# mLSTM layer on one core: the order of the opening, where two weight products stand, and the gate arithmetic in ten pieces

## The chip, the cores and the metric

The kernel runs on one core of a Trainium2 chip. The metric is device time in microseconds (us) of one execution, median over the runs shown. Engines are named as in the profile: PE (matrix products and transposes), PEld (its weight loads), DVE (vector), ACT (activation), POOL (GpSimd), SP (issues most loads).

## The reference, cut to what matters

One layer (DEPTH 1, so only the mLSTM mixer and the SwiGLU run), 2048 tokens, width 1024, 8 heads:

```
u = rmsnorm(x, mix_norm_g)
q, k, v, o_pre, if_pre = split(u @ w_in)          # 3072 columns, and 16 gate columns
gates = if_pre + b_if;  log_i = gates[:8];  log_f = log_sigmoid(gates[8:])
# per chunk: cumulated log_f, running maximum m, decay matrix, scores, state (C, n)
h = x + (rmsnorm_heads(h_mlstm) * norm_g * sigmoid(o_pre)) @ w_out
out = h + (silu(rms(h) @ w_gate) * (rms(h) @ w_up)) @ w_down
```

## The kernel before

**Arithmetic.** Every float32 matrix is kept as a high and a low part (both of a reduced float32 format): a product is three passes on PE, high x low, high x high, low x high. ACT makes the high part by a copy, DVE the low part by a subtraction. Over that lies Strassen's scheme in Winograd's form: a 2 x 2 block product takes 7 products (P1 to P7) of sums of blocks. On the side of the tokens these sums are T1 to T4 of early token tiles (0 to 3 of a half) and late ones (4 to 7).

**Halves and stages.** The tokens are done in two halves (h = 0, 1) of 8 tiles of 128. Each half: opening (norm, transposes, split), input projection (84 units, 12 groups of 7 products), the recurrence over 8 chunks, the SwiGLU's up phase, and its down phase (77 units, e = 0 to 76). The opening of half 1 follows on the down phase of half 0: rows of half 1 are normed beside units 36 to 71 (ROWS_AT), one pair is summed at unit 52 (SUMS_AT) and tiles 0 to 3 are transposed beside units 69 to 72 (TURN_AT). Half 0 has no such phase ahead of it.

**The opening.** A half has 16 "units of turning" (`turn_unit` on PE, L1726; `op_hi` on ACT, L778; `op_lo` on DVE, L1171). Units 0 to 3 turn the early tiles whole (8 transposes each). Units 4 to 15 belong to the four pairs p (early tile p, late tile 4 + p), three each: A (T1 and a late part, 8 transposes), B (T2 and T3, 8), C (T4, 4). Their sums are made by DVE (`sum_early`, L1160: two subtractions of 128x512) and POOL (`sum_late`, L626: two more). The order before is B, C, A of each pair, pair after pair (`part_of`, L374). A unit waits until the one two before it has been split by `op_lo`, since two pairs of PSUM banks take turns.

**Projection.** Unit n of the 84 is product q of group g (`unit_at`, `unit_of`, L64 to L72), with FEED = P1, P2, P6, P5, P7, P3, P4 for q = 0 to 6. Its weights come from `raw` (`proj_sums`, L1188: three steps of DVE sums), are split by `proj_hi` (ACT, L783) and `proj_lo` (DVE, L1177) into a ring of 6, and go through PE in `project(n)` (L1778, 12 matmuls of 128x512, lines 1802, 1804, 1806). P1 and P2 use tokens of units 0 to 3 alone; P6 and P7 need the B units, P5 and P3 the A units, P4 the C units. Products accumulate in PSUM: `keep_unit` (ACT, L876) and `add_unit` (DVE, L1363) copy each out before the next goes on its bank. P3 waits for the keep after P5 (`act_at(h, g, 3)`), P5 for the add after P2. Before, units 0 to 3 of the projection (P1 and P2 of groups 0 and 1) stand between the turns, then come the rest of the turns with `gates(0)` and `gates(1)` (L1810: 16 and 24 matmuls for the 16 gate columns, to banks 5 and 6), and units 4 to 83 after all of them.

**Gates.** DVE's `gate_part` (L1300) has three steps for each half t of the 1024 tokens, at projection units 6, 8, 11 and 14, 16, 19; ACT's has three more (L851) at 7, 9, 11 and 15, 17, 19. The tiles have 8 partitions x 512. Step 1 of DVE is one unbroken row of eight operations with two scans. At unit 22 the columns are transposed (`colt`).

**Order.** All orders are written out by hand; every engine runs its own list in order and waits on semaphores. DVE's order in the opening stands at L1245 to L1295 and L1372 to L1404, ACT's at L811 to L849 and L910 to L932, PE's at L1822 to L1859, POOL's at L638 to L656. In half 1 POOL's `sum_late` for pairs 1 to 3 and DVE's `sum_early` for them come after the down phase; DVE waits there for the stores of the result (L1281).

Of the kernel before, what the change touches and what calls it, by code (L numbers as in the profile page):

```python
# [5 lines left out]
F32 = mybir.dt.float32  # L6
F32R = mybir.dt.float32r
BF16 = mybir.dt.bfloat16
ALU = mybir.AluOpType
# [40 lines left out]
SUMS_AT = 52  # L50
# [13 lines left out]
def unit_at(g, q):  # L64

    if g < 2:
        return 2 * g + q if q < 2 else 2 + 5 * g + q
    return 7 * g + q
# [6 lines left out]
def act_at(h, g, i):  # L75

    n = (g + 1 if i == 1 else 3 * g + i + 1) if g < 2 else 4 * g + i
    return h * 4 * PG + n


def dve_at(h, g, i):

    n = (g + 1 if i == 1 else 2 * g + i + 1) if g < 2 else 3 * g + i
    return h * 3 * PG + n

# [6 lines left out]
def mlstm_layer(nc, x, mix_norm_g, ffn_norm_g, w_gate, w_up, w_down, w_in, b_if, norm_g, w_out, out):  # L92
# [8 lines left out]
    with ExitStack() as ctx:  # L101
# [14 lines left out]
        def small(name, shape, dt=F32):  # L116
            n = 1
            for s in shape[1:]:
# [29 lines left out]
        pkept = [[place(f"pkept{s}_{i}", r_q + (16 + 8 * s + 2 * i) * KB, [P, NB], F32) for i in range(4)]  # L148
                 for s in range(2)]
# [36 lines left out]
        def blocks(name, *runs):  # L186
# [31 lines left out]
        t2_spare = [place(f"t2_spare{i}", at, [P, NB], F32) for i, at in  # L218
                    enumerate((r_v + 24 * KB, r_v + 26 * KB, junk_at))]
        t2_first = [[t_rows0[1], t2_spare[0], t2_spare[1], t2_spare[2]],  # L220
                    [t_rows0[1], t2_spare[2], t2_spare[0], t2_spare[1]]]
# [152 lines left out]
        def part_of(stage, n):  # L374
            return ("BCA", "ABC")[stage % 2][(n - 4) % 3]

        def unit_for(stage, i, part):
            return made_of(i, ("BCA", "ABC")[stage % 2].index(part))
# [17 lines left out]
        def unit_home(stage, n, lo):  # L396
# [3 lines left out]
            p, part = (n - 4) // 3, part_of(stage, n)  # L400
# [14 lines left out]
        def t_rows(stage, p):  # L415

            h, second = stage // 2, stage % 2
# [3 lines left out]
            t2r = t2_second[p] if second else t2_first[h][p]  # L421
            return early[:, 0:NB], t2r[:, :], early[:, NB:D]

# [178 lines left out]
        def _(pool):  # L602
# [35 lines left out]
            for h in range(HALVES):  # L638
                st = 2 * h
                if h:  # L640
                    pool.wait_ge(e_lo_done, past(h * NE))
                    pool.wait_ge(drained, past(h * NE))
                nc.gpsimd.memset(if_w[:, :, :].bitcast(F32), 0.0).then_inc(prep_done, 1)
                if h == 0:
# [6 lines left out]
                    sum_late(st, 0)  # L651
                for p in range(1, 4):
                    sum_late(st, p)
# [105 lines left out]
        def _(act):  # L759
# [23 lines left out]
            def proj_hi(h, n):  # L783
# [6 lines left out]
                else:  # L790
                    act.wait_ge(p_summed, h * 4 * PG + 4 * g + {2: 2, 3: 2, 4: 4, 5: 3}[q])
# [10 lines left out]
            for h in range(HALVES):  # L802
# [7 lines left out]

                if h == 0:  # L811
                    nc.scalar.preload_act_table_set("natural_log_exp_and_others")
                    norm1_sum(0, 0)
                    norm1_sum(0, 1)
                    op_hi(0, 0)
                    norm1_sum(0, 2)
                    op_hi(0, 1)
                    norm1_sum(0, 3)
                    op_hi(0, 2)
                    proj_hi(0, 0)  # L820
                    norm1_sum(0, 4)
                    op_hi(0, 3)
                    proj_hi(0, 1)
                    norm1_sum(0, 5)
                    proj_hi(0, 2)
                    proj_hi(0, 3)
                    split_if()
                    norm1_sum(0, 6)
                    op_hi(0, 4)
                    op_hi(0, 5)  # L830
                    norm1_sum(0, 7)
                    op_hi(0, 6)
                else:
                    act.wait_ge(drained, past(h * NE - 2))
                    proj_hi(h, 0)
                    proj_hi(h, 1)
                    act.wait_ge(drained, past(h * NE - 1))
                    proj_hi(h, 2)
                    proj_hi(h, 3)
                    act.wait_ge(drained, past(h * NE))  # L840
                    act.wait_ge(p_lo_done, h * PU + 4)
                    op_hi(st, 4)
                    act.wait_ge(out_stored, h * 96)
                    act.wait_ge(last_stored, h * 64)
                    op_hi(st, 5)
                    op_hi(st, 6)
                    split_if()
                for n in range(7, OP_UNITS):
                    op_hi(st, n)  # L849
# [43 lines left out]

                def sigmoid(g, i, k):
# [15 lines left out]
                keep_unit(0, 0)  # L910
                keep_unit(1, 0)
                proj_hi(h, 4)
                proj_hi(h, 5)
                for n in range(6, 10):
                    proj_hi(h, n)
                for n in range(4, PU):
                    g, q = unit_of(n)
                    keep_unit(g, q)
                    if n + PRING < PU:
                        proj_hi(h, n + PRING)  # L920
                    if g in O_GROUPS:
# [4 lines left out]
                        if q == 6:  # L926
                            sigmoid(g, 2, 1)
                            sigmoid(g, 3, 3)
                    for t in range(2):
                        for step, at in enumerate((7, 9, 11)):  # L930
                            if n == at + 8 * t:
# [199 lines left out]
        def _(dve):  # L1131
# [56 lines left out]
            def proj_sums(h, g, step):  # L1188
# [3 lines left out]
                at = h * 4 * PG + 4 * g  # L1192
                if step == 0:
# [5 lines left out]
                    dve.wait_ge(p_summed, at + 1)  # L1199
                    nc.vector.tensor_tensor(w[:, lower, first], w[:, lower, second], w[:, lower, first], ALU.subtract)\  # L1200
                        .then_inc(p_summed, 1)
                if step == 1:
                    if g >= 2:
                        dve.wait_ge(p_lo_done, h * PU + unit_at(g, 1) + 1)
                    dve.wait_ge(p_summed, at + 2)
# [28 lines left out]
            for h in range(HALVES):  # L1234
# [9 lines left out]

                if h == 0:  # L1245
# [858 lines left out]
```

## Time and profile before

| what | value |
|---|---|
| median of 3 runs | 2276.28 us (2270.1, 2276.28, 2278.3) |
| the profiled execution | 2272.74 us, span 2271.1 us |
| mean granted clock of PE | 0.98 |
| PE busy | 2160.6 us (95%) |
| DVE, ACT, POOL busy | 64%, 41%, 12% |
| opening of half 0, first product to unit 4 | 23.6 to 70.8 us |
| opening of half 1 | 1148.5 to 1191.0 us |

The profile is of one execution. The page gives busy time by engine, forty slices, DMA, the chain of waits and groups; the trace behind it gives each instruction with its start, its duration and what it waited for.

### The profile page before, as it was taken

How to read it: one execution, taken by the hardware profiler on the slowest of the kernel's cores; microseconds unless marked ns; L12 is line 12 of the kernel's file. 1: busy time of each engine (PE TensorE's matmuls, PEld its weight loads, DVE VectorE, ACT ScalarE, POOL GpSimd, SP SyncE). 2: the span in 40 equal slices, each digit the busy share in tenths (PEclk: the TensorE clock that was granted, in tenths of full speed). 3: DMA queues.
4: the chain of work that ended last, by engine and by line, in shares of the span. 5: the costliest groups of instructions: out<-in, count | busy, mean ns of one | idle time of the engine just before them, and what ended most of it. 6: DMA issues, size and time to landing. Idle time of an engine off the chain costs nothing.

```text
span 2271.1 us, 29460 instructions
## 1 busy us (share of the span) xinstructions
PE 2160.6 (95%) x10440; PEld 1791.1 (79%) x10440; DVE 1459.3 (64%) x2274; ACT 922.6 (41%) x1670; POOL 280.4 (12%) x373
## 2 busy tenths in 40 slices
PE   5999989989999999999989999899799999999999
PEld 4778868867888888888867888688588888887887
DVE  7755456777565656579667553677766565656764
ACT  5433653334333333445434346533343333333443
POOL 3111110120010101100021111111201010101000
PEclk8999989999999999999999999899899999999999
DMA  4323372212323233864413334623032323257443
GB/s 140 96 90 112 102 263 95 97 47 74 113 93 115 92 115 127 298 228 114 149 63 107 107 104 138 218 102 103 19 112 98 111 97 111 97 179 247 148 120 117
DMA packets 200288, 281.56 MB, mean 124 GB/s; under 512 B 12912, under 2 KB 131696, under 8 KB 200176
## 3 DMA queue, kind: packets, MB, share of 16 engines
q1 hardware_dynamic: 171696, 183.07, 25.7%
q0 software_dynamic: 28480, 97.02, 12.1%
q8 instruction: 68, 1.11, 0.2%
q14 instruction: 44, 0.36, 0.0%
HBM read 197.73 MB, written 82.31 MB: 123 GB/s over the span
## 4 chain that ended last, share of the span: by engine, by line
PE 87%; DVE 7%; ACT 2%; issue 2%; DMA 1%; SPq 0%; POOL 0%; DVEq 0%; ACTq 0%; POOLq 0%
PE ps L2011 12%; PE ps L2013 12%; PE ps L2014 12%; PE ps L1802 6%; PE ps L1806 6%; PE ps L1804 6%; PE ps L2058 6%; PE ps L2062 6%; PE ps L2060 6%; PE ps L1716 2%; PE ps L1718 2%; PE ps L1717 2%; PE ps L1723 1%; PE ps L1924 1%; DVE u_lo L1174 1%
## 5 line engine op out<-in xcount | busy, mean ns | idle before, releaser
L1561 DVE TENSOR_TENSOR ring<-raw_f,ring 128x512 fp32r<-128x512 f32 x308 | 213.4, 694 | 190.0 <-ACT ring L1019 188.8
L2011 PE MATMUL ps<-u_lo,ring 128*128 128x512 f32 x704 | 275.1, 391 | 4.3 <-DVE u_lo L1174 4.3
L1019 ACT CAST ring<-raw_f 128x512 fp32r<-128x512 f32 x308 | 190.6, 622 | 212.0 <-PE ps L2014 196.8
L2013 PE MATMUL ps<-u_hi,ring 128*128 128x512 f32 x704 | 274.2, 389 | 0.0
L2014 PE MATMUL ps<-u_hi,ring 128*128 128x512 f32 x704 | 274.0, 389 | 0.0
L2058 PE MATMUL ps<-ring,ring 128*128 128x512 f32 x616 | 241.2, 392 | 3.3 <-DVE ring L1635 3.2
L2060 PE MATMUL ps<-ring,ring 128*128 128x512 f32 x616 | 240.4, 390 | 0.0
L2062 PE MATMUL ps<-ring,ring 128*128 128x512 f32 x616 | 240.2, 390 | 0.0
L2011 PE MATMUL ps<-t_op,ring 128*128 128x512 f32 x528 | 207.3, 393 | 5.9 <-DVE ring L1561 5.9
L2013 PE MATMUL ps<-t_op,ring 128*128 128x512 f32 x528 | 207.0, 392 | 0.0
L2014 PE MATMUL ps<-t_op,ring 128*128 128x512 f32 x528 | 206.9, 392 | 0.0
L1057 ACT CAST ring<-g_in 128x512 fp32r<-128x512 f32 x154 | 95.6, 621 | 222.3 <-PE ps L2062 210.3
L729 POOL DMA_DIRECT2D ops_hbm<-kept x154 | 83.3, 541 | 784.5 <-DVE kept L1654 584.9
L1629 DVE TENSOR_TENSOR ring<-g_in,ring 128x512 fp32r<-128x512 f32 x154 | 106.1, 689 | 112.7 <-ACT ring L1057 112.7
L1186 DVE TENSOR_TENSOR pring<-raw,pring 128x512 fp32r<-128x512 f32 x132 | 90.9, 691 | 128.1 <-ACT pring L798 127.3
L1802 PE MATMUL ps<-u_lo,pring 128*128 128x512 f32 x384 | 152.8, 398 | 9.0 <-ACT pkept L888 4.5
L1649 DVE TENSOR_TENSOR kept<-ps,kept 128x512 f32<-128x512 f32 x132 | 90.9, 688 | 109.3 <-PE ps L2014 109.3
L2011 PEld LDWEIGHTS ps<-u_lo,ring 128*128 128x128 f32 x704 | 132.5, 188 | 32.5 <-DVE u_lo L1174 5.1
L2014 PEld LDWEIGHTS ps<-u_hi,ring 128*128 128x128 f32 x704 | 132.3, 188 | 27.5
L2013 PEld LDWEIGHTS ps<-u_hi,ring 128*128 128x128 f32 x704 | 132.4, 188 | 27.1
L1804 PE MATMUL ps<-u_hi,pring 128*128 128x512 f32 x384 | 151.5, 395 | 0.0
L1806 PE MATMUL ps<-u_hi,pring 128*128 128x512 f32 x384 | 151.4, 394 | 0.0
(218 smaller groups left out, 4276.6 us busy)
## 6 DMA issues: line engine op xcount, KB each, us to landing
ops_hbm<-kept POOLq DMA_DIRECT2D x154, 256.0 KB, 2.4
g_in<-ops_hbm SPq DMA_DIRECT2D x154, 256.0 KB, 2.7
raw<-in_ml_w_in_dram SPq DMA_DIRECT2D x24, 1024.0 KB, 5.3
proj_hbm<-pkept POOLq DMA_DIRECT2D x96, 256.0 KB, 2.7
raw_f<-in_ffn_w_gate_dram SPq DMA_DIRECT2D x44, 512.0 KB, 4.7
raw_f<-in_ffn_w_up_dram SPq DMA_DIRECT2D x44, 512.0 KB, 4.7
b<-in_ffn_w_down_dram SPq DMA_DIRECT2D x88, 256.0 KB, 4.9
x_in<-in_x_dram SPq DMA_DIRECT2D x16, 512.0 KB, 5.9
```

The lines of the kernel that those rows point to most:

```text
L1019: nc.scalar.copy(four(ring[slot][:, 0, :]), feed_source(q, s)).then_inc(w_hi_done, 1)
L1561: nc.vector.tensor_tensor(four(ring[slot][:, 1, :]), feed_source(q, s), four(ring[slot][:, 0, :].bitcast(F32)), ALU.subtract).then_inc(w_l ...
L1629: nc.vector.tensor_tensor(ring[e % 3][:, 1, :], g_in[e % 4][:, :], ring[e % 3][:, 0, :].bitcast(F32), ALU.subtract).then_inc(ea_lo_done, 1)
L1802: pe.matmul(banks(bank), w[:, 0, now], moved(kind, 1, k), start=(fresh and k == 0), stop=False, skip_group_check=True)
L1804: pe.matmul(banks(bank), w[:, 0, now], moved(kind, 0, k), start=False, stop=False, skip_group_check=True)
L1806: last = pe.matmul(banks(bank), w[:, 1, now], moved(kind, 0, k), start=False, stop=(k == 3), skip_group_check=True)
L2011: pe.matmul(banks(bank), wh, moved(kind, 1, k), start=(fresh and k == 0), stop=False, skip_group_check=True)
L2013: pe.matmul(banks(bank), wh, moved(kind, 0, k), start=False, stop=False, skip_group_check=True)
L2014: last = pe.matmul(banks(bank), wl, moved(kind, 0, k), start=False, stop=(k == 3), skip_group_check=True)
L2058: pe.matmul(banks(bank + j), a[:, 0, now], w[:, 1, :], start=(fresh and n == 0), stop=False, skip_group_check=True)
L2060: pe.matmul(banks(bank + j), a[:, 0, now], w[:, 0, :], start=False, stop=False, skip_group_check=True)
L2062: last = pe.matmul(banks(bank + j), a[:, 1, now], w[:, 0, :], start=False, stop=(n == GROUPS - 1), skip_group_check=True)
```

## The change

Six things are changed. (1) In even stages units 4 to 15 follow FIRST_UNITS: B0, C0, B1, B2, B3, A0, A1, A2, A3, C1, C2, C3. (2) P6 of groups 0 and 1 become projection units 4 and 5 and are fed between the turns; products are issued in halves (`k0, k1`) with turns between; P5, P7, P3, P4 of group 0 are units 6 to 9, those of group 1 units 10 to 13. (3) `gates(0)` stands after unit 3, `gates(1)` after turn unit 13, into banks 1 and 7. (4) DVE's gate arithmetic is cut into ten steps; for t = 0 two are in the opening and eight at units 8 to 18, for t = 1 at units 20, 21 and 24 to 34; the columns are transposed at unit 38. (5) In half 1 the sums of pairs 1 to 3 are made at units 71, 73 and 75 of the down phase, POOL's part too. (6) Buffers: T2 tiles and `pkept` lie elsewhere; ACT and DVE drop their waits for `last_stored`; new waits on `t_made_pool` stand before `op_hi` and `op_lo` of unit 9, and keeps come earlier (`keep_first`).

```diff
-SUMS_AT = 52
+SUMS_AT = {52: 0, 71: 1, 73: 2, 75: 3}
+FIRST_UNITS = [("B", 0), ("C", 0), ("B", 1), ("B", 2), ("B", 3), ("A", 0), ("A", 1), ("A", 2), ("A", 3), ("C", 1),
+               ("C", 2), ("C", 3)]
+GATE_DVE = (0, 0, 8, 9, 10, 11, 12, 13, 14, 18)
+GATE_ACT = (0, 13, 15)
+GATE_NEXT = 16
+GATE_NEXT_DVE = (20, 21)
+GATE_NEXT_ACT = 22
+COLT_AT = 38
...
-        return 2 * g + q if q < 2 else 2 + 5 * g + q
+        return 2 * g + q if q < 2 else 4 + g if q == 2 else 3 + 4 * g + q
...
@@ POOL @@
                 if h:
+                    for p in range(1, 4):
+                        sum_late(st, p)
                     pool.wait_ge(e_lo_done, past(h * NE))
...
@@ ACT @@
+                def keep_first(g, q):
+                    act.wait_ge(turned, st * OP_UNITS + {(0, 0): 5, (1, 0): 7, (0, 2): 10, (1, 2): 11}[g, q])
+                    keep_unit(g, q)
...
+                op_hi(st, 7)
+                op_hi(st, 8)
+                proj_hi(h, 4)
+                act.wait_ge(t_made_pool, st * 8 + 8)
+                op_hi(st, 9)
+                op_hi(st, 10)
+                act.wait_ge(xn_done, st * TILES + TILES)
+                proj_hi(h, 5)
+                keep_first(0, 2)
+                op_hi(st, 11)
+                op_hi(st, 12)
+                keep_first(1, 2)
+                proj_hi(h, 6)
+                op_hi(st, 13)
+                proj_hi(h, 7)
+                gate_part(0, 0)
+                op_hi(st, 14)
+                op_hi(st, 15)
...
-                for n in range(4, PU):
+                for n in range(2, PU):
                     g, q = unit_of(n)
-                    keep_unit(g, q)
+                    if n >= 6:
+                        keep_unit(g, q)
...
@@ DVE @@
+                    op_lo(0, 4)
+                    norm1_rows(0, 6)
                     split_if()
-                    norm1_rows(0, 6)
-                    op_lo(0, 4)
+                    op_lo(0, 5)
                     sum_early(0, 2)
-                    op_lo(0, 5)
+                    add_unit(0, 1)
                     norm1_rows(0, 7)
                     op_lo(0, 6)
                     sum_early(0, 3)
+                    add_unit(1, 1)
+                    proj_sums(0, 0, 0)
+                    op_lo(0, 7)
+                    proj_sums(0, 1, 0)
+                    op_lo(0, 8)
+                    proj_lo(0, 4)
+                    dve.wait_ge(t_made_pool, st * 8 + 8)
+                    op_lo(0, 9)
...
                 op_lo(st, 10)
+                proj_lo(h, 5)
                 op_lo(st, 11)
                 op_lo(st, 12)
+                gate_part(0, 0)
+                proj_lo(h, 6)
+                gate_part(0, 1)
+                op_lo(st, 13)
                 proj_sums(h, 0, 1)
+                proj_sums(h, 0, 2)
+                proj_lo(h, 7)
                 op_lo(st, 14)
                 op_lo(st, 15)
...
@@ PE @@
-                project(0)
+                project(0, 0, 2)
                 turn_unit(st, 4)
+                project(0, 2, 4)
                 turn_unit(st, 5)
-                project(1)
-                turn_unit(st, 6)
-                turn_unit(st, 7)
-                project(2)
+                project(1, 0, 2)
+                if h:
+                    turn_unit(st, 6)
+                project(1, 2, 4)
+                project(2, 0, 2)
+                if h == 0:
+                    turn_unit(st, 6)
+                project(2, 2, 4)
+                if h:
+                    turn_unit(st, 7)
+                project(3, 0, 2)
+                project(3, 2, 4)
+                pe.wait_ge(p_dve, dve_at(h, 0, 1))
+                gates(0)
+                if h == 0:
+                    turn_unit(st, 7)
                 turn_unit(st, 8)
                 turn_unit(st, 9)
-                project(3)
+                pe.wait_ge(op_lo_done, st * OP_UNITS + 9)
+                project(4, 0, 2)
                 turn_unit(st, 10)
+                project(4, 2, 4)
                 turn_unit(st, 11)
+                project(5, 0, 2)
                 turn_unit(st, 12)
+                project(5, 2, 4)
                 turn_unit(st, 13)
+                pe.wait_ge(op_lo_done, st * OP_UNITS + 13)
+                gates(1)
                 turn_unit(st, 14)
-                gates(0)
                 turn_unit(st, 15)
-                pe.wait_ge(op_lo_done, st * OP_UNITS + OP_UNITS)
-                gates(1)
-                for n in range(4, PU):
+                pe.wait_ge(gate_dve, 2 * h * 14 + 5)
+                for n in range(6, PU):
+                    if n == unit_at(0, 6):
+                        pe.wait_ge(op_lo_done, st * OP_UNITS + OP_UNITS)
                     project(n)
```

In half 1 DVE's list has `add_product(h - 1, 6)` after `proj_lo(1)`, then op_lo 4, 5, `split_if`, `add_unit(0, 1)`, op_lo 6, `proj_sums(0)`, `add_unit(1, 1)`, op_lo 7, 8, `proj_lo(4)`, op_lo 9, `proj_sums(1)`, and goes on as shown. In the loop over units the weight sums of group 1 (steps 1 and 2) are made at unit 4, right ahead of the low part of unit 11.

## Rows read from the trace of the kernel before

**Rows 1.** The page's first part: busy us (share), instructions.

```profile
PE 2160.6 (95%) x10440; PEld 1791.1 (79%) x10440; DVE 1459.3 (64%) x2274; ACT 922.6 (41%) x1670; POOL 280.4 (12%) x373
```

**Rows 2.** The waits of PE: waiting line, releaser, total us, times, longest us.

```profile
PE ps L1723 <- DVE t_op L1174: 17.4, 11, 4.9
...
PE ps L1802 <- DVE pkept L1370: 6.6, 4, 2.4
...
PE ps L1802 <- ACT pkept L888: 4.5, 2, 2.2
```

**Rows 3.** By stretch: length, PE, PEld, DVE, ACT, POOL busy us, clock, DMA, GB/s.

```profile
23.60:70.80 47.20, 35.08 (x169) 28.76 (x170) 37.55 (x50) 18.77 (x33) 16.52 (x12) 0.89 0.07 21
...
94.00:100.00 6.00, 5.05 (x15) 4.09 (x16) 5.83 (x11) 4.01 (x8) 0.75 (x1) 0.72 0.11 34
...
1148.50:1191.00 42.50, 32.42 (x169) 27.16 (x168) 25.35 (x32) 13.93 (x20) 13.30 (x11) 0.92 0.17 56
```

**Rows 4.** PE in order of time, half 0: start, us, form [idle before, releaser].

```profile
23.61 0.79 PE L1802 MATMUL ps<-u_lo,pring 128*128 128x512 f32 x1 [2.72 <-DVE u_lo L1174]
...
70.80 0.39 PE L1802 MATMUL ps<-t_op,pring 128*128 128x512 f32 x1
71.02 0.39 PE L1804 MATMUL ps<-t_op,pring 128*128 128x512 f32 x1
...
94.94 0.54 PE L1802 MATMUL ps<-u_lo,pring 128*128 128x512 f32 x1 [2.23 <-ACT pkept L888]
95.28 0.63 PE L1804 MATMUL ps<-u_hi,pring 128*128 128x512 f32 x1
95.71 0.63 PE L1806 MATMUL ps<-u_hi,pring 128*128 128x512 f32 x1
```

**Rows 5.** The chain that ended last, 56 to 71 us: start, us, what.

```profile
56.70 3.66 PE ps L1819 x16
60.37 0.89 PE ps L1723 x8
...
63.60 7.36 PE ps L1819 x24
```

**Rows 6.** PE in order of time, end of the down phase to half 1's projection.

```profile
1134.37 0.50 PE L2058 MATMUL ps<-ring,ring 128*128 128x512 f32 x1 [0.47 <-DVE ring L1635]
...
1148.47 0.39 PE L1802 MATMUL ps<-u_lo,pring 128*128 128x512 f32 x1
...
1191.03 0.39 PE L1802 MATMUL ps<-t_op,pring 128*128 128x512 f32 x1
```

**Rows 7.** ACT in order of time: a split of 1024, and three of 512.

```profile
46.64 1.01 ACT L781 CAST u_hi<-ps 128x1024 fp32r<-128x1024 f32 x1 [1.92 <-PE ps L1723]
...
66.10 1.66 ACT L798 CAST pring<-raw 128x512 fp32r<-128x512 f32 x3 [1.80 <-DVE raw L1210]
```

**Rows 8.** DVE in order of time: half 0's opening and gates, and the down phase.

```profile
30.43 3.45 DVE L1186 TENSOR_TENSOR pring<-raw_first,pring 128x512 fp32r<-128x512 f32 x2
...
39.63 2.24 DVE L1150 SCALAR_TENSOR_TENSOR x_in<-x_in,nv,gain 128x1024 f32<-128x1024 f32 x1
...
47.69 1.22 DVE L1174 TENSOR_TENSOR u_lo<-ps,u_hi 128x1024 fp32r<-128x1024 f32 x1 [1.63 <-ACT u_hi L781]
48.83 0.68 DVE L1195 TENSOR_TENSOR raw<-raw 128x512 f32<-128x512 f32 x1
...
80.47 1.51 DVE L1312 TENSOR_SCALAR t<-ps,bias 8x512 f32<-8x512 f32 x2
82.01 1.41 DVE L1316 TENSOR_TENSOR t<-ps,t 8x512 f32<-8x512 f32 x2
...
90.41 1.19 DVE L1330 TENSOR_TENSOR_SCAN t<-not_first,t 8x512 f32<-8x512 bf16 x1
...
1131.90 1.22 DVE L1174 TENSOR_TENSOR u_lo<-ps,u_hi 128x1024 fp32r<-128x1024 f32 x1
```

**Rows 9.** POOL in order of time: the two sums of pair 3, half 0.

```profile
43.68 1.77 POOL L632 TENSOR_TENSOR x_in<-x_in 128x512 f32<-128x512 f32 x1 [2.89 <-DVE x_in L1167]
45.41 1.27 POOL L636 TENSOR_TENSOR x_in<-x_in,t_spare 128x512 f32<-128x512 f32 x1
```

More of the change, by code:

```diff
@@ L928, in _ @@
                             sigmoid(g, 3, 3)
+                    if n == GATE_NEXT_ACT:
+                        gate_part(1, 0)
                     for t in range(2):
-                        for step, at in enumerate((7, 9, 11)):
-                            if n == at + 8 * t:
+                        for step in (1, 2):
+                            if n == GATE_ACT[step] + GATE_NEXT * t:
                                 gate_part(t, step)
@@ L1245, in _, with add_unit @@
+                def add_unit(g, q):
+                    k = pkept[g % 2]
+                    x_bank, v_bank = 2 * (g % 3), 2 * (g % 3) + 1
+                    kept_, bank, after = {1: (0, v_bank, 1), 4: (2, x_bank, 3), 5: (1, v_bank, 2)}[q]
+                    dve.wait_ge(p_fed, h * PU + unit_at(g, q) + 1)
+                    dve.wait_ge(p_act, act_at(h, g, after))
+                    nc.vector.tensor_tensor(k[kept_][:, :], banks(bank), k[kept_][:, :], ALU.add).then_inc(p_dve, 1)
                 if h == 0:
@@ L1286, in _ @@
-                op_lo(st, 8)
-                op_lo(st, 9)
-                proj_sums(h, 0, 0)
+                    proj_sums(h, 0, 0)
+                    add_unit(1, 1)
+                    op_lo(st, 7)
+                    op_lo(st, 8)
+                    proj_lo(h, 4)
+                    dve.wait_ge(t_made_pool, st * 8 + 8)
+                    op_lo(st, 9)
+                    proj_sums(h, 1, 0)
                 op_lo(st, 10)
+                proj_lo(h, 5)
                 op_lo(st, 11)
@@ L1373, in _ @@
-                proj_lo(h, 4)
-                proj_lo(h, 5)
-                proj_sums(h, 0, 2)
-                proj_lo(h, 6)
-                proj_lo(h, 7)
-                add_unit(1, 1)
-                proj_lo(h, 8)
-                proj_sums(h, 1, 0)
-                proj_sums(h, 1, 1)
-                proj_lo(h, 9)
-                for n in range(4, PU):
+                for n in range(2, PU):
                     g, q = unit_of(n)
-                    if q in (1, 4, 5):
+                    if n >= 6 and q in (1, 4, 5):
@@ L1395, in _ @@
                             proj_sums(h, g, 2)
+                    if n in GATE_NEXT_DVE:
+                        gate_part(1, GATE_NEXT_DVE.index(n))
                     for t in range(2):
-                        for step, at in enumerate((6, 8, 11)):
-                            if n == at + 8 * t:
+                        for step in range(2, 10):
+                            if n == GATE_DVE[step] + GATE_NEXT * t:
                                 gate_part(t, step)
-                    if n == 24:
+                    if n == COLT_AT + 2:
                         dve.wait_ge(colt_turned, h + 1)
@@ L1743, in turn_unit @@
                     return
[L1744 removed]
+                p, part = pair_of(stage, n), part_of(stage, n)
                 rows = rows_of(stage, 4 + p)
@@ L1799, in project @@
                     w = pring[n % PRING]
-                    for k in range(4):
+                    for k in range(k0, k1):
                         now = slice(k * P, k * P + P)
@@ L1818, in gates @@
                     for i, (k, m) in enumerate(steps):
-                        last = pe.matmul(banks(5 + t), if_w[:, k, :], m, start=(i == 0), stop=(i == len(steps) - 1))
+                        last = pe.matmul(banks(gate_bank(t)), if_w[:, k, :], m, start=(i == 0), stop=(i == len(steps) - 1))
                     last.then_inc(if_done, 1)
```

286 lines of the change are left out of this document (138 added, 148 removed).

## Prediction

> **What bounds the kernel now.** I read the busy shares first: PE is busy 95% of the span, DVE 64% [rows 1]. So the end is set by PE nearly everywhere, and only the 5% in which it idles or runs at its lower clock can be won without less arithmetic. The list of PE's waits then says where the idle time is: 17.4 us wait for `op_lo` at the transposes, and 6.6 and 4.5 us at products for `add_unit` and for `keep_unit` after P5 [rows 2]. The stretches tell where: 12.1 us idle in half 0's opening (47.20 less 35.08), 10.1 in half 1's (42.50 less 32.42) [rows 3]. Beside the idling stands the clock: 0.89 and 0.92 of full in the openings, 0.72 from 94 to 100 us behind a 2.23 us stall [rows 3, 4].
>
> The price of PE's work: one matmul every 0.227 us (70.80, then about 71.03) and 0.43 us at the lower level, 1.2 of 2.4 GHz (95.28 to 95.71) [rows 4]. A unit of 12 is 2.73 us; `gates` cost 16 x 0.227 = 3.65 and 24 x 0.227 = 5.45 us; eight transposes 0.89, four 0.44 us [rows 5]. Units 4 to 15 of turning (80 transposes) cost 8.8 us. An opening holds four products, these turns and both gates: 10.9 + 8.8 + 9.1 = 28.8 us. It took 70.80 - 23.61 = 47.2 us in half 0 and 1191.03 - 1148.47 = 42.6 us in half 1 [rows 4, 6]. So 18.4 and 13.8 us are lost: the idle time above, the rest lower clock (`gates(1)` took 7.36 instead of 5.45 [rows 5]).
>
> **Part 1, order of the opening.** The change gives PE two more products (5.45 us) to put between turns, and puts `gates(0)` where the sums of pairs 2 and 3 are waited for. What limits is then the handshake PE, ACT (1.01 for 1024, 0.55 for 512 [rows 7]), DVE (1.22; other ops of 512 about 0.7, in a row 0.6 [rows 8]). I go through DVE's list in its new order, with these durations.
>
> Half 0 until DVE's fourth `proj_lo` (33.88) is as before. `op_lo(4)` follows at once, done 35.1; PE, which has gone from 23.61 through turns 4 and 5, units 0 and 1 and half of unit 2 by 33.6, waits 1.5 us for it. Turn 6, the rest of unit 2 and unit 3 end at 40.15, `gates(0)` at 43.85, turn 7 at 44.75. Meanwhile DVE does row 6, `split_if`, op_lo 5, `sum_early(2)` (39.15), `add_unit(0,1)` (39.75: the gates do not wait), row 7 (2.24 beside POOL [rows 8]), op_lo 6 (43.7), `sum_early(3)` (45.05). POOL's sum for B3 needs 1.77 us [rows 9] from 44.35: turn 8 starts at 46.15, 1.4 us idle. Then DVE has an add, two weight sums (the first beside POOL, 1.7) and op_lo 7: 49.3, so turn 9 waits 2.3 us. Two more sums, op_lo 8 and `proj_lo(4)`: 52.5, and product 4 waits 2.25 us. So much idling should leave PE at its lower level for product 4 and a turn, 2.1 us. Product 5 waits 0.6 us for its low part, `gates(1)` 0.5 us for op_lo 12: they run 63.45 to 68.95, and after turns 14 and 15 unit 6 starts at 69.85.
>
> DVE is by then behind: after op_lo 12 (63.4) it has gate step 0 (1.51), `proj_lo(6)`, step 1 (1.41 + 0.7 [rows 8]), op_lo 13, two sums, `proj_lo(7)` (70.8), op_lo 14, 15 (73.1), low parts 8, 9, 10 and the two sums of group 1 (76.3). ACT in order waits for these sums before high part 11 (76.9), and only then keeps unit 6 (77.45). P3, unit 8, waits for that keep: PE would be there at 69.85 + 5.45 = 75.3 and starts at 77.5, 2.2 us late. This is the new stall that I name for the change. Before, unit 8 started at 70.80 + 4 x 2.73 = 81.7. Half 0's opening gains 4.2 us, not the 12 of its idle time.
>
> Half 1 by the same steps, without POOL beside it, counted from the last product of the down phase (1148.47): op_lo 4 at 1153.9, no stall there; unit 3 ends at 1162.6, `gates(0)` at 1166.25, turns 8 and 9 at 1168.05. Product 4 waits for op_lo 8 (ACT, DVE behind turn 8) and `proj_lo(4)`: 1170.1, 2.0 us idle; 0.6 at product 5, 0.5 before `gates(1)`; unit 6 at 1186.25. The same keep holds unit 8 from 1191.7 to 1194.15. Before, unit 8 started at 1191.03 + 10.9 = 1201.9. Gain 7.8 us.
>
> Bounds: at most all of the loss goes, 18.4 + 13.8 = 32.2 us. From the other side, if each transposing unit after the eighth is late by a full exchange (turn 0.9, split 1.01 + 1.22) with nothing between, the openings gain nothing (0 to -3 us). I take 12.0, nearest to the rows since each step has its duration there.
>
> **Part 2, gates in ten steps.** DVE's step 1 is one row of eight operations, 6.3 us with a scan of 1.19 us [rows 8]; behind it stand low parts and adds, and ACT, which waits for it, has the keep after P5 behind. Now the largest piece is 1.3 us per unit of 2.73, beside at most one add, one low part and two sums (0.6 to 0.7 each, 3.4 us at unit 8). I count units 8 to 22 through: P4 and P5 of each group find their adds 1.5 us or more ahead. So 6.6 + 4.5 = 11.1 us of waits go [rows 2], and the lower clock behind them: 0.28 of 6 us is 1.7, by matmuls 8 x 0.2 = 1.6; there are three such stretches (94, 122, 1242 us), 4.4 us in all. Against that, the new stall at unit 8 (2.2 and 2.45 us) is of the same length as those after which three times of four the clock fell: I charge 1.5 us twice, 3.0. Sum 11.1 + 4.4 - 3.0 = 12.5. Ends: all stays (0), all goes and no clock falls (15.5).
>
> `gate_part(0)` needs bank 1 from `add_unit(0,1)`, and unit 6 needs it back after gate step 1 (66.0 or so): both in time. The new waits on `t_made_pool` ahead of op_hi 9 and op_lo 9 would hold the whole lists of ACT and DVE, but POOL is done at 47.4 (43.7 + two sums, beside DVE's later start) and they come there at 52: nothing. `colt` moves from unit 22 to 38; its readers come after unit 84, so nothing. The weight load for group 2 is released by low part 9 (74.3), lands about 6 us later, at 80.6, when ACT comes to it: nothing, at most 1 us.
>
> **Part 3, sums in the down phase.** At unit 71 DVE already has row 7 and op_lo 2; PE waits there 0.47 us for low parts of unit 72 [rows 6]. Now two subtractions (1.4 us) stand ahead of op_lo 2 (started 1131.90 [rows 8]), and POOL's two sums run beside the low parts of unit 72: an operation with both inputs in SBUF then takes 1.72 instead of 0.69 (3.45 for two [rows 8]), one with an input in PSUM does not (`op_lo`). Unit 72: +1.4 and +0.5 us. Unit 74 comes behind the sums of pair 2 and beside POOL's, 1142.9 against a PE that is there at 1141.75: +1.2; some 0.4 of the waits of before are in it already. Pair 3's sums fall beside unit 76, which has a unit in hand. Cost 2.7 us, once; between 0 (if the ring's lead covers it) and 6 us (3 pairs at 2 x 1.03 us of contention, none covered).
>
> The Trainium skill ("SBUF — State Buffer", section "Who interferes with whom") says that a DVE instruction with two inputs in SBUF and a GpSimd instruction that reads SBUF take turns on one read port, held for a whole instruction. It speaks against this part of the change, where three pairs of POOL sums move beside low parts that bound PE. By its rule each POOL operation delays one DVE operation by up to its length, 1.3 us, six in all 7.8 us, had nothing covered them; by the rows it is 1.03 us each. The trace agrees on kind (1.72 beside POOL, 0.69 alone).
>
> **Sum.** 12.0 + 12.5 - 2.7 = 21.8 us off the profiled execution's 2272.74: 2250.9. The three runs have a median of 2276.28, 3.5 above it; on their footing it is 2254.5, rounded 2254.
>
> **Rivals.** (a) The openings are bound by DVE's order and gain nothing, only the stalls in the projection go: 12.5 - 2.7 = 9.8, time 2266. For it: DVE is busy 37.6 of 47.2 us in half 0's opening [rows 3] and gets the gate steps and sums on top. Against: half 1 has no POOL beside it and 25.4 us busy in 42.5. Chance 0.15. (b) The stall at unit 8 does not come, since ACT or DVE run a little ahead, and the clock stays up: 4.65 + 3.0 + 2 more, time 2245. For it: it hangs on DVE being late by 2 us after some 25 operations. Chance 0.15. (c) Slower. The ten steps, each a place in DVE's order with waits, sit ahead of adds that PE waits for; 18 in the loop of each half, 36 in all. The rest of the sum gains 21.8, so from (21.8 + 11.4)/36 = 0.9 us of delay for each the kernel is slower by over 0.5%; at a scan's 1.19 us each it is 43 less 21.8, time 2297. Against: in these units DVE idled for 1 to 2 us between low parts. Chance 0.03. (d) Sums in the down phase cost 6 us and a fall of the clock (1.5): 2254 + 4.8 = 2259; chance 0.12. (e) The named case, 0.55.
>
> **Numbers.** The named case alone lies within 2248 to 2261. The range reaches to most of (a) and (b): 2244 to 2267. No change is within 0.5%, 11.4 us, about what a measurement can tell here: the runs before spread over 8 us. Slower by more: (c) and a bit, 0.03. Within: two thirds of (a), as 9.8 us is below 11.4, 0.10. Faster 0.87.
>
> **What would show it.** Right: PE starts unit 6 near 70 us and unit 8 near 77.5 with a wait on the keep of unit 6; half 1's opening from the last down product to unit 8 takes 46 instead of 53.5 us; `gates(1)` takes 5.5 us in both; waits on `add_unit` after unit 8 are gone; 2 to 4 us of new waits on DVE's ring in the last six down units. Wrong: idle time over 8 us between turn 7 and product 4, waits of PE on `add_unit` near units 10 to 34, or a clock below 0.9 in the openings.

## The result, and the profile after

The changed kernel takes 2252.36 us (median of 4 runs, 2248.2 to 2253.3) against 2274.88 for the kernel before, run beside it. The ratio is 0.9903, with a 95% interval of 0.9887 to 0.9919: 1.0% faster, where 2254 us was forecast. Its profiled execution took 2252.24 us; the forecast on that footing was 2250.9. First the page's first part, the engines' busy us, share and instructions, as in [rows 1]:

```profile
PE 2156.8 (96%) x10440; PEld 1787.7 (79%) x10440; DVE 1462.9 (65%) x2274; ACT 923.2 (41%) x1670; POOL 282.5 (13%) x373
```

The work is the same; DVE and POOL are 3.6 and 2.1 us busier, which is on balance contention between them (below). The waits of PE, as in [rows 2] (waiting line, releaser, total us, times, longest):

```profile
...
PE ps L2127 <- DVE ring L1683: 7.1, 5, 2.9
...
PE ps L1771 <- DVE t_op L1213: 6.2, 7, 2.2
...
PE ps L1851 <- DVE t_op L1213: 4.1, 2, 2.1
PE ps L1851 <- ACT pkept L866: 4.0, 2, 2.0
```

`op_lo` is now line 1213, a product 1851 to 1855, a turn 1771, a down product 2127 to 2131. The turns wait 6.2 us for `op_lo` in place of 17.4, but 4.1 us of waits for it now stand at product 4; the 6.6 us of waits for `add_unit` are gone; the waits for a keep are now those of unit 8; and the waits for DVE's ring in the down products have grown to 7.1 us. The stretches, columns as in [rows 3]: half 0's opening up to unit 8, a place in which PE stood before, and half 1's opening.

```profile
23.60:79.20 55.60, 45.56 (x216) 36.57 (x217) 45.38 (x59) 23.37 (x41) 16.95 (x12) 0.91 0.09 27
...
94.00:100.00 6.00, 6.00 (x29) 4.95 (x28) 3.14 (x9) 3.48 (x6) 1.50 (x2) 1.00 0.30 90
...
1146.00:1192.00 46.00, 40.60 (x210) 33.44 (x209) 29.17 (x39) 19.22 (x30) 3.73 (x5) 0.99 0.17 53
```

From 94 to 100 us PE is busy for all 6.00 us at a granted clock of 1.00; before it was 5.05 us at 0.72 [rows 3]. Half 0's opening still idles for 10.0 us. PE in order of time shows at which units (start, us, form, idle before and releaser):

```profile
23.62 0.80 PE L1851 MATMUL ps<-u_lo,pring 128*128 128x512 f32 x1 [2.72 <-DVE u_lo L1213]
...
35.09 0.66 PE L1771 MATMUL ps<-ident,t_first 128*128 128x128 f32 x4 [1.17 <-DVE t_op L1213]
...
46.26 0.63 PE L1771 MATMUL ps<-ident,t_first 128*128 128x128 f32 x4 [1.45 <-POOL x_in L649]
...
49.53 0.66 PE L1771 MATMUL ps<-ident,t_rows 128*128 128x128 f32 x4 [2.21 <-DVE t_op L1213]
...
52.63 0.76 PE L1851 MATMUL ps<-t_op,pring 128*128 128x512 f32 x1 [2.01 <-DVE t_op L1213]
53.19 0.63 PE L1853 MATMUL ps<-t_op,pring 128*128 128x512 f32 x1
...
56.89 0.74 PE L1851 MATMUL ps<-t_op,pring 128*128 128x512 f32 x1
...
58.62 1.03 PE L1771 MATMUL ps<-ident,x_in 128*128 128x128 f32 x8
60.20 0.50 PE L1851 MATMUL ps<-t_op,pring 128*128 128x512 f32 x1 [0.54 <-DVE pring L1225]
...
61.72 1.04 PE L1771 MATMUL ps<-ident,x_in 128*128 128x128 f32 x8
...
65.12 0.50 PE L1869 MATMUL ps<-u_lo,if_w 128*128 128x512 f32 x1 [0.54 <-DVE u_lo L1213]
...
71.51 0.48 PE L1851 MATMUL ps<-u_lo,pring 128*128 128x512 f32 x1
...
76.82 0.39 PE L1855 MATMUL ps<-t_op,pring 128*128 128x512 f32 x1
79.21 0.47 PE L1851 MATMUL ps<-u_lo,pring 128*128 128x512 f32 x1 [2.01 <-ACT pkept L866]
...
1127.38 0.50 PE L2127 MATMUL ps<-ring,ring 128*128 128x512 f32 x1 [2.94 <-DVE ring L1683]
...
1134.42 0.50 PE L2127 MATMUL ps<-ring,ring 128*128 128x512 f32 x1 [1.31 <-DVE ring L1683]
...
1143.26 0.39 PE L1851 MATMUL ps<-u_lo,pring 128*128 128x512 f32 x1
...
1189.44 0.47 PE L1851 MATMUL ps<-u_lo,pring 128*128 128x512 f32 x1 [2.01 <-ACT pkept L866]
...
1191.08 0.63 PE L1851 MATMUL ps<-u_lo,pring 128*128 128x512 f32 x1
```

From 53.19 the matmuls follow each other at 0.43 us (their rows then show 0.63, at the full level 0.39): the lower level behind three waits, as forecast. At 79.21 and 1189.44 stands the forecast stall at unit 8. A wait costs PE more than its row says: at 76.82 the next matmul was due 0.23 us later, at 77.05, and came at 79.21, which is 2.16 us and not 2.01; with the slower start behind it (the next came at 79.52, 0.31 us on) it is 2.24.

Where the time went, by such starts in both traces (us):

| stretch | before | after | difference | forecast |
|---|---|---|---|---|
| half 0, first product to unit 8 | 58.07 | 55.59 | -2.5 | -4.2 |
| half 0, unit 8 to last product | 216.96 | 207.52 | -9.4 | } -12.5 |
| half 1, unit 8 to last product | 215.40 | 209.14 | -6.3 | } in both |
| half 1, first product to unit 8 | 53.44 | 46.18 | -7.3 | -7.8 |
| turn of tile 2 in the down phase (1129.24; 1119.77) to half 1's first product | 19.23 | 23.49 | +4.3 | +2.7 |
| sum | | | -21.2 | -21.8 |

The profiled executions differ by 20.5 us. The rest of the span is two stretches that no edit aims at: half 0's last product to the turn of tile 2, and half 1's last product to the end. Over the ten profiled kernels of this document they vary by themselves, from 830.4 to 835.2 and from 848.0 to 853.8 us. So the worth of an edit is read below from its stretches, since a whole time can't show a few us of it.

### The profile page after: what moved, and what is told of

It is laid out like the page before. It is cut to its first block, busy times and chain, and to the rows that moved or that the text cites. A ratio compares the mean times of both kernels' runs of the same rounds, so it can differ in the third digit from the quotient of the medians.

```text
span 2250.6 us, 29475 instructions
## 1 busy us (share of the span) xinstructions
PE 2156.8 (96%) x10440; PEld 1787.7 (79%) x10440; DVE 1462.9 (65%) x2274; ACT 923.2 (41%) x1670; POOL 282.5 (13%) x373
## 3 DMA queue, kind: packets, MB, share of 16 engines
q0 software_dynamic: 28480, 97.02, 12.3%
## 4 chain that ended last, share of the span: by engine, by line
PE 87%; DVE 7%; DMA 2%; issue 2%; ACT 2%; SPq 0%; ACTq 0%; DVEq 0%
PE ps L2080 12%; PE ps L2082 12%; PE ps L2083 12%; PE ps L1851 6%; PE ps L1855 6%; PE ps L1853 6%; PE ps L2127 5%; PE ps L2131 5%; PE ps L2129 5%; PE ps L1764 2%; PE ps L1766 2%; PE ps L1765 2%; PE ps L1993 1%; PE ps L1771 1%; DMA g_in<-ops_hbm 1%
```

## The experiments

Each is the changed kernel with one edit, if nothing else is said. "Openings" are the stretches from a half's first product to its unit 8 (55.6 and 46.2 us in the changed kernel), "projections" those from there to its last product (207.5 and 209.1).

**The sums back out of the down phase.**

```
-SUMS_AT = {52: 0, 71: 1, 73: 2, 75: 3}
+SUMS_AT = {52: 0}
 ...                       (DVE, half 1's opening)
                     proj_lo(h, 0)
+                    sum_early(st, 1)
 ...
                     op_lo(st, 5)
+                    sum_early(st, 2)
 ...
                     proj_sums(h, 0, 0)
+                    sum_early(st, 3)
```

POOL's sum of pair 1 goes back ahead of its wait for the drained output, those of 2 and 3 behind its memset of `if_w`.

> The changed kernel with its part 3 undone: pairs 1 to 3 of half 1 are summed in the opening again (pair 1 behind low part 0, pair 2 behind op_lo 5, pair 3 behind the weight sums), the new unit order stays. The stretch from PE's turn of tile 2 in the down phase to half 1's first product was 19.2 us in the kernel before and 23.5 in the changed one. Theory (the sums and POOL beside the last low parts cost 4.2 us and bring nothing, for DVE idles in half 1's opening): 19.2 to 19.7 us, half 1's opening to unit 8 stays at 46.2 us within 1 us, time 2248. Rival (the sums are needed early; back in the opening they hold turns 6 to 8): the stretch is 19.2 but the opening takes 4 us or more longer, time 2252 or above.

Measured: 2243.61 us (2242.7 to 2247.6), ratio 0.9888 (0.9871 to 0.9904) to the kernel before at 2271.35. Turn of tile 2 to first product 19.25 us instead of 23.49, as before the change; half 1's opening 46.22, unmoved. The time is 4 us under its forecast and 8.7 under the changed kernel's 2252.36, but the kernel before, run beside it, was 3.5 us faster too; by the ratios the gain is 3.4 us, with overlapping intervals. What the edit is worth is the 4.2 us of its stretch. DVE of the changed kernel shows why (start, us, form): low parts of units 72 and 74, one alone and three beside POOL:

```profile
1124.97 0.68 DVE L1677 TENSOR_TENSOR ring<-g_in,ring 128x512 fp32r<-128x512 f32 x1
1125.57 1.76 DVE L1683 TENSOR_TENSOR ring<-b,ring 128x512 fp32r<-128x512 f32 x1
...
1130.91 1.78 DVE L1677 TENSOR_TENSOR ring<-g_in,ring 128x512 fp32r<-128x512 f32 x1
1132.61 1.76 DVE L1683 TENSOR_TENSOR ring<-b,ring 128x512 fp32r<-128x512 f32 x1
```

And POOL of the changed kernel, the same stretch:

```profile
1130.34 1.80 POOL L649 TENSOR_TENSOR x_in<-x_in 128x512 f32<-128x512 f32 x1 [3.56 <-DVE x_in L1206]
```

The same low part takes 0.68 alone and 1.76 us beside POOL. So this part of the change costs 4.2 us in the down phase and gives half 1's opening nothing.

**POOL's sums behind the down phase's low parts.**

```
                 if h:
+                    pool.wait_ge(e_lo_done, past(h * NE))
                     for p in range(1, 4):
                         sum_late(st, p)
-                    pool.wait_ge(e_lo_done, past(h * NE))
```

DVE's subtractions stay in the down phase.

> The changed kernel, but POOL makes its sums of pairs 1 to 3 only when the last low part of the down phase is made; DVE's own sums stay at units 71, 73, 75. Theory (most of the 4.2 us is POOL beside DVE: five low parts at 1.76 instead of 0.68 us): no low part there takes over 0.8 us, PE's three waits (2.94, 1.31, 0.20 us) shrink to about 1.9, 0 and 0, the stretch from the turn of tile 2 to half 1's first product is 20.7 to 21.3 us instead of 23.5. Rival (it is DVE's own 1.4 us at each of three units and their place in the order): 22.5 us or more, the wait at unit 74 stays over 0.8 us.

Measured: 2249.93 us in one run. PE of this kernel:

```profile
1126.24 0.50 PE L2127 MATMUL ps<-ring,ring 128*128 128x512 f32 x1 [1.83 <-DVE ring L1683]
...
1127.71 0.63 PE L2131 MATMUL ps<-ring,ring 128*128 128x512 f32 x1
...
1141.58 0.39 PE L1851 MATMUL ps<-u_lo,pring 128*128 128x512 f32 x1
...
1163.93 0.47 PE L1851 MATMUL ps<-t_op,pring 128*128 128x512 f32 x1 [2.13 <-DVE t_op L1213]
...
1165.05 0.63 PE L1853 MATMUL ps<-t_op,pring 128*128 128x512 f32 x1
```

The same product 4 of half 1 in the changed kernel:

```profile
1165.00 0.47 PE L1851 MATMUL ps<-t_op,pring 128*128 128x512 f32 x1 [2.13 <-DVE t_op L1213]
...
1166.01 0.39 PE L1853 MATMUL ps<-t_op,pring 128*128 128x512 f32 x1
```

And DVE of the kernel of this experiment:

```profile
1129.76 0.69 DVE L1677 TENSOR_TENSOR ring<-g_in,ring 128x512 fp32r<-128x512 f32 x1
...
1137.00 3.51 DVE L1225 TENSOR_TENSOR pring<-raw_first,pring 128x512 fp32r<-128x512 f32 x2 [1.37 <-ACT pring L816]
```

With POOL away each low part is 0.69 us and the waits of the last down units fall from 4.45 to 1.83 us, 0.47 of which were there before the change [rows 6]: 2.6 us are contention with POOL, 1.4 the two subtractions in DVE's order. The stretch, 21.82 us, is above the forecast 20.7 to 21.3, since the clock fell behind the wait: from 1127.28 eight matmuls stand at the lower level, some 1.6 us. POOL's sums now meet low parts of half 1 (two take 3.51 us), and its opening grows by 2.0 us to 48.2. Most of that is not contention: product 4 starts 22.35 us after the first product in place of 21.74, so 0.6 us reach PE. The other 1.4 lie behind product 4, where the lower level came after a wait of 2.13 us that the changed kernel has too, without the fall.

**Gates in big pieces again.**

```
-GATE_DVE = (0, 0, 8, 9, 10, 11, 12, 13, 14, 18)
+GATE_DVE = (0, 0, 8, 8, 8, 8, 8, 8, 8, 11)
-GATE_ACT = (0, 13, 15)
+GATE_ACT = (0, 9, 11)
-GATE_NEXT_DVE = (20, 21)
+GATE_NEXT_DVE = (21, 22)
-GATE_NEXT_ACT = 22
+GATE_NEXT_ACT = 23
```

> The changed kernel with part 2 undone as far as its order allows: DVE's gate steps 2 to 8 stand in one piece at unit 8 (t = 0) and 24 (t = 1), step 9 at 11 and 27, the next gates' first two at 21 and 22, ACT's at 9, 11, 23, 25, 27. Theory (one unbroken piece of about 6 us holds adds and keeps): PE waits again for a keep or an add in units 9 to 34, 2 to 2.5 us twice in each half, 8 to 10 us in all, with lower clock behind most: 2260 to 2266. Rival (the stalls of before came from gates and projection starting together, at a time when low parts were short, not from the size of the piece): under 3 us of such waits, 2252 to 2255.

Measured: 2266.57 us (2263.4 to 2271.6, 10 runs), ratio 0.9978 (0.9968 to 0.9988), where the changed kernel has 0.9903: three quarters of the gain are gone. The projections take 217.05 and 216.78 us, 9.5 and 7.6 more. PE, DVE and a stretch of this kernel:

```profile
91.92 0.47 PE L1851 MATMUL ps<-u_lo,pring 128*128 128x512 f32 x1 [1.06 <-ACT pkept L866]
...
138.19 0.76 PE L1851 MATMUL ps<-t_op,pring 128*128 128x512 f32 x1 [5.18 <-DVE pkept L1360]
```

```profile
136.64 0.68 DVE L1343 TENSOR_TENSOR t<-cols,nm_end 8x512 f32<-8x512 f32 x1
137.36 0.69 DVE L1360 TENSOR_TENSOR pkept<-ps,pkept 128x512 f32<-128x512 f32 x1
```

```profile
130.00:150.00 20.00, 14.82 (x54) 11.68 (x53) 13.21 (x22) 7.00 (x12) 2.25 (x3) 0.83 0.15 42
```

DVE works through one piece from 130.5 to 137.3 us with the add behind it; PE waits 5.18 us for that add and gets a granted clock of 0.83 over the 20 us. All such waits are 6.2 and 5.9 us in the two halves, more than the 8 to 10 forecast for both. This is the stall that ten steps remove, though the kernel before had it in three smaller waits in each half (2.23, 0.89 and 2.43 us in half 0), where its pieces stood at other units. The experiment is no exact return to it: it brings back 17.1 us, where the ten steps had won 15.7.

**The keep of unit 6 ahead of ACT's high part 11.**

```
-                    if n >= 6:
+                    if n >= 7:
                         keep_unit(g, q)
+                    if n == 5:
+                        keep_unit(0, 3)
                     if n + PRING < PU:
                         proj_hi(h, n + PRING)
```

> The changed kernel, but ACT keeps unit 6 ahead of high part 11, which waits for DVE's weight sums of group 1; nothing else is moved. Theory (the stall of 2.01 us before unit 8 in both halves is ACT's order alone): the stall goes in both halves, below 0.3 us, and is not found again at units 9 to 14; half 0's stretch from the first product to unit 8 is 53.6 instead of 55.6 us; time 2248, 4 us less. Rival (DVE is late anyway, and the next wait stands right behind): PE waits 1 us or more at one of units 8 to 14 for a low part, an add or a keep, and the gain is under 2 us.

Measured: 2250.24 us (2245.5 to 2252.4), ratio 0.9914 (0.9898 to 0.9931); openings 53.15 and 44.00, so -2.4 and -2.2; projections 208.40 and 208.41. ACT of the changed kernel first, then ACT and PE of this one:

```profile
77.96 0.62 ACT L816 CAST pring<-raw 128x512 fp32r<-128x512 f32 x1 [2.32 <-DVE raw L1248]
78.49 0.58 ACT L866 COPY pkept<-ps 128x512 f32<-128x512 f32 x1
```

```profile
75.79 0.57 ACT L866 COPY pkept<-ps 128x512 f32<-128x512 f32 x1
```

```profile
80.91 0.47 PE L1853 MATMUL ps<-t_op,pring 128*128 128x512 f32 x1 [0.73 <-DVE pkept L1362]
```

The mechanism is as forecast: the keep (78.49) stood behind a high part that waited 2.32 us for DVE's sums; put ahead it runs at 75.79 and the stall is gone. But 0.73 us come back one unit later, at an add in DVE's list, so truth lies between theory and rival. By stretches 4.4 us are left (-2.4, -2.2, +0.9, -0.7), 1.6 of them the fall of the clock that half 1's projection no longer has. The whole time doesn't resolve it: the medians are 2.1 us apart with their runs overlapping, and by the ratios (0.9914 against 0.9903) there is no gain at all.

**Gates(0) back behind the turns.** Part 1 changed the place of `gates(0)`, too.

```
-                pe.wait_ge(p_dve, dve_at(h, 0, 1))
-                gates(0)
 ...
+                pe.wait_ge(p_dve, dve_at(h, 0, 1))
                 pe.wait_ge(op_lo_done, st * OP_UNITS + 13)
+                gates(0)
                 gates(1)
```

> The changed kernel, but gates(0) stands right ahead of gates(1), as before the change. Theory (in half 0 its 3.65 us lie in the wait for the sums of pairs 2 and 3): PE's wait before turn 8 grows from 1.45 to about 5 us and half 0's stretch from the first product to unit 8 from 55.6 to 59 us; in half 1, where no sum is waited for, turn 9 waits for op_lo 7 behind the add of unit 3, 1 us or so, and the stretch goes from 46.2 to 47 to 48 us. Rival (the gates only take the place of other waits): both stretches within 1 us of the changed kernel.

Measured: 2260.6 us in one run; openings 59.01 and 48.39, 3.4 and 2.2 longer. PE of this kernel:

```profile
46.74 1.08 PE L1771 MATMUL ps<-ident,t_first 128*128 128x128 f32 x4 [4.83 <-POOL x_in L649]
50.01 1.11 PE L1771 MATMUL ps<-ident,t_rows 128*128 128x128 f32 x4 [1.33 <-DVE t_op L1213]
```

In half 0 the 3.65 us of gates filled a wait for the sums that is now 4.83 us; the next turn waits 1.33 instead of 2.21 us, and product 4 starts 28.98 us after the first product instead of 29.01, so the gates cost nothing there. The rest of part 1, with the new stall at unit 8 in it, has no gain left in half 0: 2.5 us in all, 3.4 from this. In half 1 the place fills nothing: without the gates product 4 starts 3.6 us earlier (18.11 instead of 21.74 us after the first product), and they cost the same behind. The 2.2 us there are 1.6 for the clock, which fell behind product 4 (7.05 us from it to product 5 instead of 5.47), and 0.6 for a longer stall at unit 8, 2.59 us.

**Products 4 and 5 whole, behind the turns.** Here PE has nothing to do between the turns.

```
-                project(4, 0, 2)
                 turn_unit(st, 10)
-                project(4, 2, 4)
                 turn_unit(st, 11)
-                project(5, 0, 2)
                 turn_unit(st, 12)
-                project(5, 2, 4)
                 turn_unit(st, 13)
+                project(4)
+                project(5)
```

ACT's `keep_first(0, 2)` moves behind its high part 12.

> The changed kernel, but P6 of groups 0 and 1 are fed behind turn 13 instead of between turns 10 to 13. Theory (two products of 2.73 us fill waits for the split of the A units): each of the turns 11 to 13 waits 1.5 us or so for op_lo, 3 to 4 us in each half, while product 4 needs no wait of its own (2 us back): 2 to 6 us more in all, 2254 to 2258. Rival (the order B before A alone is what pays, the filling brings nothing): 2250 to 2253.

Measured: 2253.09 us (2249.4 to 2255.8), ratio 0.9921 (0.9902 to 0.9941), level with the changed kernel; openings 54.74 (-0.9) and 47.08 (+0.9). PE of this kernel:

```profile
52.54 3.92 PE L1771 MATMUL ps<-ident,x_in 128*128 128x128 f32 x16 [0.54 <-DVE t_op L1213]
56.84 1.10 PE L1771 MATMUL ps<-ident,x_in 128*128 128x128 f32 x8 [0.38 <-DVE u_lo L1213]
58.82 0.66 PE L1771 MATMUL ps<-ident,x_in 128*128 128x128 f32 x4 [0.88 <-DVE u_lo L1213]
```

Here the theory that filling the turns pays is wrong: bare, the turns wait in pieces of 0.4 to 0.9 us in half 0 (1.8 in all) and of 0.6 to 1.5 in half 1 (4.2), but product 4 does not wait 2.01 and 2.13 us for `op_lo` 8, and product 5 and `gates(1)` don't wait either. The two balance.

**DVE's weight sums behind its operand units, half 0.**

```
                     add_unit(1, 1)
+                    op_lo(0, 7)
                     proj_sums(0, 0, 0)
-                    op_lo(0, 7)
-                    proj_sums(0, 1, 0)
                     op_lo(0, 8)
                     proj_lo(0, 4)
 ...
                     op_lo(0, 9)
+                    proj_sums(0, 1, 0)
```

> The changed kernel, in half 0 only: DVE's op_lo 7 ahead of the weight sums of group 0, those of group 1 behind op_lo 9. Theory (the waits at turn 9, 2.21 us, and at product 4, 2.01 us, are DVE's weight sums, the first pair of them drawn out by POOL): turn 9 starts at 47.2 instead of 49.5, product 4 at 50.5 to 51 instead of 52.6, half 0's stretch to unit 8 is 53.5 to 54 instead of 55.6 us. Rival (POOL's sums and the exchange set it): product 4 not before 52.2.

Measured: 2250.42 us in one run; half 0's opening 52.85, 2.7 shorter. PE of this kernel:

```profile
46.78 0.63 PE L1771 MATMUL ps<-ident,t_first 128*128 128x128 f32 x4 [1.43 <-POOL x_in L649]
...
50.98 0.47 PE L1851 MATMUL ps<-t_op,pring 128*128 128x512 f32 x1 [2.17 <-DVE t_op L1213]
...
51.82 0.63 PE L1851 MATMUL ps<-t_op,pring 128*128 128x512 f32 x1
```

The wait of 2.21 us at turn 9 was two weight sums ahead of `op_lo` 7. It is gone, and product 4 starts 26.85 us after the first product instead of 29.01, 2.2 us earlier. The wait before product 4 stays (2.17 us), and the clock still falls behind it, from 51.82 on. Half 1, which the edit doesn't touch, took 47.78 us in this execution instead of 46.18, since the clock fell there behind the same wait of 2.13 us: so much can one opening differ by the clock alone.

**Together.** The sums back, the keep early and the weight sums behind, with `add_unit(0, 4)` ahead of DVE's low part 11 (against the 0.73 us at unit 9) and, in half 1, turn 8 ahead of `gates(0)`:

```
+                    if n == 5:
+                        add_unit(0, 4)
-                    if n >= 6 and q in (1, 4, 5):
+                    if n >= 6 and n != 7 and q in (1, 4, 5):
 ...
+                if h:
+                    turn_unit(st, 8)
                 pe.wait_ge(p_dve, dve_at(h, 0, 1))
                 gates(0)
                 if h == 0:
                     turn_unit(st, 7)
-                turn_unit(st, 8)
+                    turn_unit(st, 8)
```

> The changed kernel with five edits: sums of pairs 1 to 3 back in the opening (4.2 us in the down phase, measured); ACT's keep of unit 6 ahead of high part 11 and DVE's add of unit 7 ahead of low part 11 (2.0 us in each half); in half 0 op_lo 7 ahead of the weight sums and group 1's sums behind op_lo 9 (2.0 us); in half 1 turn 8 ahead of gates(0) (2.1 us). Theory (each stall is an order on ACT or DVE, and they add): 4.2 + 4.0 + 2.0 + 2.1 = 12.3 us under the changed kernel, 2240; with the 8.7 us of the sums_back run as the base 2237. Rival (the handshake of PE, ACT and DVE sets the opening, and a stall that goes is found again at the next unit): no more than sums_back, 2244.

Measured: 2233.74 us (2232.3 to 2240.5), ratio 0.9839 (0.982 to 0.9858): 1.6% below the kernel before, where the changed one is 1.0% below. The two openings in the stretches of this kernel:

```profile
24.10:73.20 49.10, 43.71 (x216) 35.95 (x217) 42.74 (x57) 21.87 (x37) 16.51 (x12) 1.00 0.05 17
...
1133.10:1175.10 42.00, 40.43 (x217) 33.80 (x216) 31.16 (x43) 17.89 (x27) 10.86 (x10) 1.00 0.17 57
```

They take 49.1 and 42.0 us, 6.5 and 4.2 less than in the changed kernel, at a granted clock of 1.00 (half 0's was 0.91), and idle for 5.4 and 1.6 us. The projections are 207.4 in both halves and the down stretch is 19.24. That is 6.5 + 4.2 + 0.1 + 1.7 + 4.3 = 16.8 us by stretches, and 18.5 by the profiled executions, where 12.3 were forecast. Most of the surplus is the clock. In half 0 product 4 still waits 2.21 us, but the level holds behind it, and product 5 starts 5.46 us after product 4 instead of 7.57; behind nearly the same wait it fell in the experiment above. That is 2.1 of the 6.5 us, and no edit aims at them. Another 1.6 are the fall in half 1's projection, which is gone with the stall at unit 8.

## Why the prediction was right

**The sum.** -21.2 us by stretches against -21.8: the sign, the size and the named case (e) hold. Three terms are off, and nearly cancel: the gain of the openings was put 2.2 us too high, that of the gates 3.2 too low, the cost in the down phase 1.6 too low. That the sum came within 1 us is luck.

**Openings: 9.8 instead of 12.0.** The walk through DVE's list put the waits at the right units and nearly at the right size: turn 6 1.17 (1.5), turn 8 1.45 (1.4), turn 9 2.21 (2.3), product 4 at 52.63 after 2.01 (52.5 after 2.25), `gates(1)` 0.54 (0.5). The step that failed lies between product 4 and `gates(1)`: 12.5 us, where I had 10.95. By my own prices 24 product matmuls (5.45), 28 transposes (3.1), the two waits (1.1) and the lower clock (2.1) are 11.75, so 0.8 was a slip of addition. The other 0.7 is the price of changing between products and turns: I had six matmuls of a half product at 1.36 us and eight transposes at 0.89. Behind a turn the half products take 1.73 (56.89 to 58.62), 1.52 (60.20 to 61.72) and 1.47 us, 0.6 more in all, and three turns take 0.2 more together. The stall at unit 8 came, 2.01 us by its row in both halves and 2.16 by the starts (2.2 and 2.45), and by the cause named: the early keep removes it. Rival (a) is out, as half 0 gained 2.5 and half 1 7.3; (b) too.

**Gates in ten steps: 15.7 instead of 12.5.** This lies above the upper end that I had given, 15.5. All 11.1 us of waits went. The projections before took 216.96 and 215.40 us and the floor without a wait is 207.5, so 17.3 stood there and 6.2 beside the waits. The starts of the matmuls part these: some 24 of them stood at the lower level, 4.5 us, much as the 4.4 that I had taken. The other 1.7 I had put at nothing: mostly six waits, each of which costs some 0.24 us more than its row says, as at unit 8 above. I also charged two new clock falls of 1.5 behind the stall at unit 8. It fell once, in half 1 (1.6 us). The big pieces bring 9.5 and 7.6 us back. Rival (c), that each of 36 small pieces delays PE, has nothing for it: from unit 8 on PE waits for nothing in either projection (207.49 busy of 207.50 us in half 0).

**Down phase: +4.3 instead of +2.7.** Forecast were waits of 1.9 us at unit 72, on top of the 0.47 of before, and of 1.2 at unit 74, 3.1 in all, of which some 0.4 were there before; they are 2.94 and 1.31, with 0.20 at unit 76, 4.0 more than before. At unit 72 the rows give 0.47 (already there before), 1.4 for two subtractions and 1.08 for one low part beside POOL: 2.95. I had counted 0.5 of contention there. The mechanism was right, its size too small; rival (d), with 6 us, was too large. The Trainium skill ("SBUF — State Buffer", section "Who interferes with whom") lets a DVE instruction with two inputs in SBUF and a GpSimd instruction that reads SBUF contend for one shared read interface, an exclusive lock. The rows agree in kind, at 1.08 us more for each of five low parts, 5.4 in all, of which 2.6 reached PE. The forecast worst case, six low parts each delayed by a whole POOL addition, 7.8 us, did not come: five low parts were hit and not six, at 1.08 us each, and of these 5.4 us the ring's lead covered half.

**What stays open.** Half 1's opening gained 7.3 us. With `gates(0)` put back it is 2.2 less, but 1.6 of that is a fall of the clock behind product 4, which three other kernels show with `gates(0)` in its new place, so only 0.6 us is shown to be its place. The rest, 5.1 to 6.7 us, belongs to the new order of the turns and to the products between them; products 4 and 5 between the turns are worth 0.9 of it. That the sums' place is no part of it is shown (46.22 with them back); the order of the turns was not tried by itself.

## What to carry to other kernels

Walk the in-order list of the engine that feeds the bound one, with row durations, and look for the instruction behind which a small release is queued: here most stalls over 1 us were a keep, an add or a low part behind something that nobody was waiting for, and moving it cost little. Read a single opening with care: a wait of 2 us with or without the lower level behind it is worth 1.4 to 2.1 us more or less. Cut long side work into pieces shorter than the lead of the bound engine. Filling a wait with work pays only if the filled work does not itself need what is late.

## What the runs showed of the hardware

A DVE operation on 128x512 with both inputs in SBUF takes 0.69 us alone and 1.76 beside a POOL one, which itself goes from 1.27 [rows 9] to 1.77: the pair costs each side. With one input in PSUM it is not slowed: `op_lo` takes 1.22 us at 1123.83 while POOL adds from 1123.28 on, as it does alone. A single wait of about 2 us may or may not be followed by the lower of PE's two levels: 2.01 us at 79.21 was not, the same 2.01 us at 1189.44 was (rows of 0.63 us from 1190.7 on, 1.6 us lost). Over the kernels here that have this stall at 2.0 to 2.1 us, the level fell behind it in half 1 in three of six (the changed kernel, the first and the seventh experiment) and in half 0 in none; at 2.59 us, with `gates(0)` back, it fell in both. Behind the 2.13 us at product 4 of half 1 it held in three kernels and fell in three. Why it falls in one and not in the other is not shown; in a forecast it is open, and worth nearly as much as the stall.
